# Strassen's seven products on a quarter of K in seven blocks of the last FFN

## The chip, the cores and the metric

The kernel runs on one core of a Trainium2 chip. The metric is the device time of one execution in microseconds, the median of a few runs. The engines are TensorE (PE in the profile, its weight loads PEld), VectorE (DVE), ScalarE (ACT), GpSimd (POOL) and SyncE (SP), which here only issues DMAs. Each works through its own list of instructions in order, and they wait for each other on semaphores.

## The reference

Two layers of a transformer trunk on 256 tokens with 2048 features in float32. Each layer has a token mixer and a SwiGLU FFN with D_FF = 5632. The change touches the FFN of the second layer, and in it the two products with `w1` and `w3`:

```python
def _swiglu(h, w1, w3, w2):
    return (jax.nn.silu(h @ w1) * (h @ w3)) @ w2

for i in range(DEPTH):
    ...
    h = x * (1.0 + sc_f) + sh_f
    y = _swiglu(h, ffn_w1[i], ffn_w3[i], ffn_w2[i])
    x = _layer_norm(DEEPNORM_ALPHA * x + (1.0 + g_f) * y, ln2_g[i], ln2_b[i])
```

## The kernel before

Every product of float32 matrices is made of three products of rounded parts: a matrix is split into a high part (`hi`, type fp32r) and what is left (`lo`), and `hi*hi + lo*hi + hi*lo` is summed in PSUM. The activations are split once. The weights come in **units** of 256 rows of K and 512 columns (512 KB, 128 partitions x 1024 elements), and each goes through a line of stations:

- SP loads it into one of five slots of `raw` (L492), when VectorE has done with the unit five before it (`lo_ready`).
- ScalarE copies it into `whi`, the high part (L710). The rings `whi` and `wlo` have five slots too, so the split of a unit waits until TensorE has used the unit five before it (`units_used`).
- VectorE subtracts: `wlo = raw - whi` (L1167).
- TensorE uses it (`unit`, L1862 and L1868): 2 chunks of K x 2 halves of the tokens x 3 products, 12 matmuls of 128x128 by 512, each with its own weight load.

VectorE and ScalarE count how far TensorE is in `pl.pe`: `units(1)` adds one and splits units until five are ahead. An instruction that comes after `units(n)` in their lists therefore stands behind the split of the unit four ahead of the last one counted.

The FFN takes the 5632 columns in 11 blocks of 512, in two passes (6 and 5 blocks). In a block, 8 units of `w1` are accumulated into one pair of PSUM banks (a bank for each half of the tokens) and 8 units of `w3` into the next; two pairs take turns (`pl.block % 2`), and `pair_read` tells TensorE that a pair was read. After the `w1` half ScalarE applies Silu out of PSUM (L1025); after the `w3` half VectorE multiplies (L1684) and transposes (L1261). SP stores the result to HBM and reads it back by token (L554, L564), ScalarE and VectorE split it (L773, L1266). After each pass follow the units of `ffn_w2` on the transposed `u`, four column blocks, each read by VectorE (L1308, L1299). VectorE also makes the adaLN vectors (`ada`, L1204), one reduction of 2048 elements after every third unit; POOL loads their weights. The last of them fall into block 3 of the second layer's FFN.

Of the kernel before, what the change touches and what calls it, by code (L numbers as in the profile page):

```python
# [7 lines left out]
F32 = mybir.dt.float32  # L8
F32R = mybir.dt.float32r
I32 = mybir.dt.int32  # L10
ALU = mybir.AluOpType
# [59 lines left out]

TOTAL = sum(PROJ) + 1 + 2 * (4 * PAIRS + 3 * D_FF // P * 4 // UC)
LAST_DOWN = TOTAL - 4 * FF_PASSES[-1] * 4 // UC

ADA_HEAD = 2 * KC
# [105 lines left out]
def trunk(nc, A, rows, u_store, qk_store, out):  # L181
# [75 lines left out]
    c_bc = new("c_bc", [P, D])  # L257
    ada_w = new("ada_w", [P, 2, D])
    raw = new("raw", [P, RING, UNIT])
    whi = new("whi", [P, RING, UNIT], F32R)  # L260
# [85 lines left out]
    with ExitStack() as ctx:  # L346
# [14 lines left out]
        ada_half_done = sem("ada_half_done")  # L361
        raw_in = [sem(f"raw_in{i}") for i in range(RING)]
        ln_in = sem("ln_in")
# [77 lines left out]
        piece_summed = sem("piece_summed")  # L441
        piece_out = sem("piece_out")

        block = ctx.enter_context(nc.Block())
# [15 lines left out]
        def split_lo(n):  # L460
            return end_lo[:, n - (TOTAL - STASH), :] if n >= TOTAL - STASH else wlo[:, n % RING, :]

        def ends(layer):
# [8 lines left out]
        def _(sp):  # L472
# [14 lines left out]
            def load(source):  # L487

                s = pl.unit % RING
                if pl.unit >= RING:  # L490
                    sp.wait_ge(lo_ready, pl.unit - RING + 1)
                sp.dma_start(raw[:, s, 0:source.shape[-1]], source).then_inc(raw_in[s], 16)  # L492
                pl.unit += 1
# [64 lines left out]
            def u_back(l, i):  # L558
# [3 lines left out]
                for a in range(QUADS):  # L562
                    for t in range(T):
                        sp.dma_start(rows_of(l, i)[a * QUAD:(a + 1) * QUAD, t, :, :],  # L564
                                     u_store[b % 2][:, :, t, a, :].rearrange("q x s -> x q s")
                                     ).then_inc(u_moved[b % 2], 16)

            def load_ffn(l):
                first = 0
                for nb in FF_PASSES:  # L570
                    for i in range(first, first + nb):
                        if (l, i) == (0, 0):
# [109 lines left out]
        def _(act):  # L682
            pl = Place()

            def widths():
                for layer in range(LAYERS):
                    for k in range(PROJ[layer]):
                        yield UC * unit_width(layer, k)
                        if layer == 1 and k == PAIRS - 1:
                            yield KC * H  # L690
                    for _ in range(4 * PAIRS):
                        yield UNIT
                    for _ in range(3 * D_FF // P * 4 // UC):
                        yield UNIT
            width = list(widths())

            def split():

                s, n = pl.unit % RING, width[pl.unit]
                act.wait_ge(raw_in[s], 16 * (pl.unit // RING + 1))  # L700
                if pl.unit >= TOTAL - STASH:
                    act.wait_ge(units_used, LAST_DOWN)
                elif pl.unit >= RING:
                    act.wait_ge(units_used, pl.unit - RING + 1)
                if pl.unit == narrow:
                    nc.scalar.activation(f_weights(s)[:, :, 0, :], raw[:, s, 0:n].rearrange("p (c n) -> p c n", c=KC),
                                         ACT.Copy).then_inc(hi_ready, 1)
                    pl.unit += 1
                    return
                nc.scalar.activation(split_hi(pl.unit)[:, 0:n], raw[:, s, 0:n], ACT.Copy).then_inc(hi_ready, 1)  # L710
                pl.unit += 1
# [285 lines left out]
            def w_o():  # L997
                units(2 + 2 * PAIRS - SPLIT)
                pl.block += 4

            def ffn(l):
                units(PAIRS - SPLIT if l > 0 else 3)
                first = 0
                for n, nb in enumerate(FF_PASSES):
                    for i in range(nb):
                        silu = silu_of(l, n, i)
                        if (l, n, i) == (0, 0, 1):
# [19 lines left out]
                        if i > 0:  # L1027
                            u_high(l, n, first + i - 1)
                        units(2 if (l, n, i) == (0, 0, 0) else PAIRS)
                        if (n, i) == (0, nb - 1):  # L1030
# [105 lines left out]
        def _(dve):  # L1136
            pl = Place()
            total = sum(PROJ) + 1 + 2 * (4 * PAIRS + 3 * D_FF // P * 4 // UC)

# [9 lines left out]
            def chain(ins):  # L1149
                mark(ins)  # L1150
                own()

            def split():

                s = pl.unit % RING
                n = KC * H if pl.unit == narrow else UNIT
# [3 lines left out]
                if pl.unit == narrow:  # L1160
                    nc.vector.tensor_tensor(f_weights(s)[:, :, 1, :],
                                            raw[:, s, 0:n].rearrange("p (c n) -> p c n", c=KC),
                                            f_weights(s)[:, :, 0, :].bitcast(F32),
                                            ALU.subtract).then_inc(lo_ready, 1)
                    pl.unit += 1
                    return
                nc.vector.tensor_tensor(split_lo(pl.unit)[:, 0:n], raw[:, s, 0:n],  # L1167
                                        split_hi(pl.unit)[:, 0:n].bitcast(F32),
# [47 lines left out]

            def units_with_ada(n, spare=0):

                for k in range(n):
                    units(1)  # L1220
                    if pl.pe % 3 == 0 and k < n - spare:
                        ada()
# [406 lines left out]
            def w_o(layer):  # L1629
# [10 lines left out]
                units(PAIRS - SPLIT - (1 if layer == 0 else 0))  # L1640

            def ffn(l):
                if l > 0:
                    units(PAIRS - SPLIT - T)
                first = 0
                for n, nb in enumerate(FF_PASSES):
                    last = n == len(FF_PASSES) - 1
                    for i in range(nb):
                        if (l, n, i) == (0, 0, 1):
                            units(1)  # L1650
# [20 lines left out]
                        elif (n, i) != (0, 0):  # L1671
                            units_with_ada(PAIRS)
                        pl.block += 1
                        if i > 0:
                            u_low(l, n, first + i - 1)
                        if (l, n, i) == (0, 0, 0):
                            units(1)
                        else:
                            units_with_ada(PAIRS, 2)
                        dve.wait_ge(units_used, pl.pe)  # L1680
# [155 lines left out]
        def _(pe):  # L1836
# [290 lines left out]
            def w_o(layer):  # L2127
# [11 lines left out]
                split_end(parts[PAIRS - SPLIT:], 2 * layer)  # L2139

            def ffn(l):
                made = l * U_BLOCKS
                for n, nb in enumerate(FF_PASSES):
                    for i in range(nb):
                        if (n, i) == (0, 0):
                            norm_turn(2 * l)
# [210 lines left out]
```

## Time and profile before

| | |
|---|---|
| timed runs, median (lowest to highest of 3) | 2195.85 us (2192.31 to 2196.93) |
| profiled execution: its span, first to last instruction | 2191.0 us |
| the profiled execution's own time around the span | not given by the page |
| TensorE busy, of the span | 2139.0 us (98%), 9557 matmuls |
| VectorE busy | 1596.9 us (73%) |
| ScalarE busy | 990.1 us (45%) |
| mean granted TensorE clock | 0.998 |

The page counts an engine as busy while an instruction of it runs; matmuls overlap, so their durations (0.39 us) are longer than their distance. Idle time before an instruction is put down to the engine that released it. The rows below are of the last FFN, from about 1465 us to the end, but for those on the clock, which are of the first 110 us.

### The profile page before, as it was taken

How to read it: one execution, taken by the hardware profiler on the slowest of the kernel's cores; microseconds unless marked ns; L12 is line 12 of the kernel's file. 1: busy time of each engine (PE TensorE's matmuls, PEld its weight loads, DVE VectorE, ACT ScalarE, POOL GpSimd, SP SyncE). 2: the span in 40 equal slices, each digit the busy share in tenths (PEclk: the TensorE clock that was granted, in tenths of full speed). 3: DMA queues.
4: the chain of work that ended last, by engine and by line, in shares of the span. 5: the costliest groups of instructions: out<-in, count | busy, mean ns of one | idle time of the engine just before them, and what ended most of it. 6: DMA issues, size and time to landing. Idle time of an engine off the chain costs nothing.

```text
span 2191.0 us, 24820 instructions
## 1 busy us (share of the span) xinstructions
PE 2139.0 (98%) x9557; PEld 1744.3 (80%) x9557; DVE 1596.9 (73%) x1792; ACT 990.1 (45%) x1291; POOL 105.1 (5%) x208
## 2 busy tenths in 40 slices
PE   5799999999999999999999999999999999999999
PEld 2378887888888888888788888878888888888887
DVE  6789999777777777778877666878775555455566
ACT  1077646444443444443544455554444433444443
POOL 2101100000000000000000000000000000000000
PEclk9999999999999999999999999999999999999999
DMA  9999997889998898999589788958987765666773
GB/s 387 418 364 362 363 388 285 276 292 341 337 340 319 320 340 322 318 350 361 193 287 331 264 273 282 338 175 290 332 295 226 234 194 191 214 212 213 219 239 124
DMA packets 177064, 635.90 MB, mean 290 GB/s; under 512 B 20385, under 2 KB 51377, under 8 KB 150705
## 3 DMA queue, kind: packets, MB, share of 16 engines
q1 hardware_dynamic: 147298, 427.93, 56.0%
q0 software_dynamic: 27792, 201.34, 24.6%
q10 hardware_dynamic: 1856, 5.04, 0.6%
q8 instruction: 76, 1.25, 0.2%
q14 instruction: 42, 0.34, 0.0%
HBM read 616.37 MB, written 17.86 MB: 289 GB/s over the span
## 4 chain that ended last, share of the span: by engine, by line
PE 86%; DMA 6%; DVE 6%; ACT 2%; issue 1%; POOL 0%; ACTq 0%; SPq 0%; DVEq 0%; POOLq 0%
PE ps L1862 53%; PE ps L1868 27%; PE ps L1879 3%; DMA gate<-in_ada_w 3%; DMA raw<-in_mla_w_o 1%; DVE wlo L1167 1%; DMA ada_head<-in_ada_w 1%; DVE ada_w L1204 1%; DVE gate L1204 1%; DMA ada_w<-in_ada_w 1%; DMA raw<-in_mla_w_uv 1%; PE ps L2091 0%; ACT whi L710 0%; DVE ada_head L1204 0%; PE ps L2121 0%
## 5 line engine op out<-in xcount | busy, mean ns | idle before, releaser
L1167 DVE TENSOR_TENSOR wlo<-raw,whi 128x1024 fp32r<-128x1024 f32 (+1 forms) x717 | 867.1, 1216 | 513.8 <-ACT whi L710 512.7
L710 ACT ACTIVATE whi<-raw 128x1024 fp32r<-128x1024 f32 (+1 forms) x717 | 756.1, 1056 | 1033.8 <-PE ps L1868 952.4
L1862 PE MATMUL ps<-whi,hT_hi 128*128 128x512 f32 x1880 | 585.7, 393 | 1.5 <-DVE hT_lo L1595 1.5
L1862 PE MATMUL ps<-whi,hT_lo 128*128 128x512 f32 x1880 | 579.5, 389 | 0.0
L1868 PE MATMUL ps<-wlo,hT_hi 128*128 128x512 f32 x1880 | 502.7, 389 | 0.0
L1862 PEld LDWEIGHTS ps<-whi,hT_lo 128*128 128x128 f32 x1880 | 352.9, 188 | 74.0
L1868 PEld LDWEIGHTS ps<-wlo,hT_hi 128*128 128x128 f32 x1880 | 352.9, 188 | 73.7
L1862 PEld LDWEIGHTS ps<-whi,hT_hi 128*128 128x128 f32 x1880 | 350.1, 188 | 72.9 <-DVE hT_lo L1595 2.0
L1204 DVE CUSTOM_DVE_ANT_0 ada_w<-ada_w,c_bc,cols 128x2048 f32<-128x2048 f32 x145 | 339.8, 2345 | 16.4 <-ACT c_bc L1050 8.4
L1862 PE MATMUL ps<-whi,uT_hi 128*128 128x512 f32 x656 | 202.0, 389 | 0.0
L1862 PE MATMUL ps<-whi,uT_lo 128*128 128x512 f32 x656 | 201.9, 389 | 0.0
L1868 PE MATMUL ps<-wlo,uT_hi 128*128 128x512 f32 x656 | 175.3, 389 | 0.0
L1862 PEld LDWEIGHTS ps<-whi,uT_lo 128*128 128x128 f32 x656 | 123.1, 188 | 25.6
L1862 PEld LDWEIGHTS ps<-whi,uT_hi 128*128 128x128 f32 x656 | 123.1, 188 | 25.6
L1868 PEld LDWEIGHTS ps<-wlo,uT_hi 128*128 128x128 f32 x656 | 123.1, 188 | 25.5
L655 POOL DMA_DIRECT2D ada_w<-in_ada_w x145 | 76.8, 530 | 1289.9 <-DVE mod L1204 1289.1
L2204 PE MATMUL ps<-down_w,h 128*128 128x512 f32 x128 | 64.8, 652 | 28.2 <-ACT h L1063 28.2
L2204 PEld LDWEIGHTS ps<-down_w,h 128*128 128x128 f32 x128 | 25.2, 208 | 57.0 <-ACT h L1063 30.9
L1204 DVE CUSTOM_DVE_ANT_0 ada_head<-ada_head,c_bc,cols 128x2048 f32<-128x2048 f32 x16 | 37.5, 2351 | 10.6 <-DMA ada_head<-in_ada_w 10.3
L1063 ACT ACTIVATE h<-ps,mod 128x256 f32<-128x256 f32 x16 | 8.9, 561 | 74.2 <-DVE mod L1204 54.4
L917 ACT ACTIVATE p_sb<-p_sb,pinv 128x128 f32<-128x128 f32 x64 | 25.7, 452 | 27.9 <-DVE pinv L1623 27.9
L1879 PE MATMUL ps<-whi,hT_hi 128*128 128x512 f32 x72 | 29.8, 414 | 3.3 <-issue 1.6
(274 smaller groups left out, 1470.0 us busy)
## 6 DMA issues: line engine op xcount, KB each, us to landing
raw<-in_ffn_w SPq DMA_DIRECT2D x528, 512.0 KB, 4.7
ada_w<-in_ada_w POOLq DMA_DIRECT2D x145, 1024.0 KB, 7.6
raw<-in_fox_w_in SPq DMA_DIRECT2D x96, 512.0 KB, 5.3
ada_head<-in_ada_w POOLq DMA_DIRECT2D x16, 1024.0 KB, 20.3
raw<-in_mla_w_o SPq DMA_DIRECT2D x32, 512.0 KB, 8.6
raw<-in_fox_w_o SPq DMA_DIRECT2D x32, 512.0 KB, 5.5
gate<-in_ada_w POOLq DMA_DIRECT2D x12, 1024.0 KB, 9.0
ada_low<-in_ada_w POOLq DMA_DIRECT2D x10, 1024.0 KB, 10.4
```

Source lines behind the costliest of these rows:

```text
L655: pool.dma_start(ada_buffer(n), A["ada_w"][l, q, c]).then_inc(ada_in[ADA_SLOT[n]], 16)
L710: nc.scalar.activation(split_hi(pl.unit)[:, 0:n], raw[:, s, 0:n], ACT.Copy).then_inc(hi_ready, 1)
L917: ins = nc.scalar.activation(p_sb[:, g % 2, a:b], p_sb[:, g % 2, a:b], ACT.Copy, scale=pinv[:, g % 2, t:t + 1])
L1063: nc.scalar.activation(h32[:, c, :], ps[:, 4 + c % 2, 0:S], ACT.Identity, scale=mod[:, SC_A, c:c + 1], bias=mod[:, SH_A, c:c + 1]).then_in ...
L1167: nc.vector.tensor_tensor(split_lo(pl.unit)[:, 0:n], raw[:, s, 0:n], split_hi(pl.unit)[:, 0:n].bitcast(F32), ALU.subtract).then_inc(lo_rea ...
L1204: nc.vector.tensor_tensor_reduce(w, w, c_bc[:, :], 1.0, adab_col[:, q, c:c + 1], ALU.mult, ALU.add, mod[:, q, c:c + 1]).then_inc(ada_done, 1)
L1862: nc.tensor.matmul(ps[:, 2 * pair + t, 0:width], a[:, t * P:(t + 1) * P], w_hi, start=(first and c == 0 and a is hi), stop=False)
L1868: ins = nc.tensor.matmul(ps[:, 2 * pair + t, 0:width], hi[:, t * P:(t + 1) * P], w_lo, start=False, stop=(end and c == UC - 1))
L1879: ins = nc.tensor.matmul(ps[:, 2 * pair + t, :], a[:, t * P:(t + 1) * P], w, start=(first and c == 0 and a is hi), stop=(end and c == UC - 1))
L2204: ins = nc.tensor.matmul(ps[:, 2 * which + t, :], h32[:, c, t * P:(t + 1) * P], w[:, which * LORA:(which + 1) * LORA], start=(c == 0), sto ...
```

## The change

In blocks 4 to 10 of the second layer's FFN (the last two of the first pass, all five of the second), the first quarter of K (512 of 2048 rows, two units of `w1` and two of `w3`) is computed by Strassen's scheme. Seen as a 2x2 of blocks, the token halves are rows, the two K units columns of the left matrix; `B11`, `B21` (of `w1`) and `B12`, `B22` (of `w3`) make the right one. Seven products of one token half by one unit take the place of eight. The left sums `S1` to `S4` are made once (`mix_inputs`, in block 3), in the buffer of the adaLN weights, and split by ScalarE and VectorE. The right sums `T1` to `T4` are made in every block by VectorE (`operand_sum`), two units ahead, in the raw slot of one of their terms, and then split like any unit. A block so has 19 units in place of 16: 7 operand units of 6 matmuls and 12 plain units of 12 for the other three quarters of K.

The seven products and the rest need all eight PSUM banks: 0 to 3 for `B11`, `T1`, `T2`, `T3`, the pair 4 and 5 for the `w1` side (with `B21`, `T4` and the plain units), the pair 6 and 7 for the `w3` side (with `B22` and the plain units). ScalarE copies bank 0 and 1 out, VectorE adds the single products together, adds the pairs (left: L1862, right: L1866), ScalarE applies Silu, VectorE multiplies and transposes. New semaphores tell TensorE which bank was read: `first_copied`, `fifth_copied`, `sixth_read`, `left_done`, `right_read`.

Four more raw slots (`raw_more`) lie where `c_bc` and the adaLN weights were; their loads wait for `mix_ready`. The adaLN reductions are made earlier: after every second unit in the first half of block 3, and to the end of block 2. The raw slots are given out by a table (`RAW_SLOT`, `RAW_FREE`), so loads run up to ten units ahead.

```diff
+FAST_FROM = 4
+FAST_BLOCKS = range(FAST_FROM, sum(FF_PASSES))
+OPERANDS = {"B11": (W1, 0), "B12": (W3, 0), "B21": (W1, 1), "B22": (W3, 1)}
+SUM_ON_DVE = {"T1": ("B11", "B12"), "T3": ("B12", "B22"), "T2": ("B11", "B22"), "T4": ("B11", "B21")}
+LEAD = 2
+    return ([("B11", 0), ("B22", 0), ("B21", 0)] + w1[:3] + [("T1", 0), ("T3", 0)] + w1[3:]
+            + [("T2", 0)] + w3[:3] + [("T4", 0)] + w3[3:])
...
@@ SP
+                n = pl.unit
+                if RAW_FREE[n]:
+                    sp.wait_ge(lo_ready, RAW_FREE[n])
+                if RAW_SLOT[n] >= RING:
+                    sp.wait_ge(mix_ready, 1)
+                sp.dma_start(raw_of(n)[:, 0:source.shape[-1]], source).then_inc(raw_in[RAW_SLOT[n]], 16)
...
+            def load_fast(first, i):
+                for n, (kind, j) in enumerate(FAST_UNITS):
+                    if kind in ONTO:
+                        pl.unit += 1
+                        continue
...
+                    load(A[name][1, i * PAIRS + which])
...
+                    if i > first and n == U_OUT_AFTER:
+                        u_out(1, i - 1)
+                    if i > first and n == U_BACK_AFTER:
+                        u_back(1, i - 1)
...
@@ ScalarE
+            def fast_block(n, i):
+                b = i - FAST_FROM
+                units(AT["B11"] + 4)
+                act.wait_ge(units_used, pl.pe - 4)
+                act.wait_ge(u_flipped, U_BLOCKS + i)
+                nc.scalar.activation(silu_all[:, 0, :], ps[:, 0, :], ACT.Copy).then_inc(first_copied, 1)
+                units(AT["T1"] - AT["B11"] - 4)
+                act.wait_ge(units_used, pl.pe)
+                nc.scalar.activation(u[:, 1, :], ps[:, 1, :], ACT.Copy).then_inc(fifth_copied, 1)
...
+                act.wait_ge(left_done, b + 1)
+                nc.scalar.activation(silu_all[:, :, :], silu_all[:, :, :], ACT.Silu).then_inc(fast_silu, 1)
...
@@ VectorE
+            def operand_sum(n):
...
+                if kind == "T1":
+                    dve.wait_ge(raw_in[slot["B12"]], 16 * loads)
+                onto, other = (raw_tile(slot[name]) for name in SUM_ON_DVE[kind])
+                nc.vector.tensor_tensor(onto, onto, other, ALU.add).then_inc(sum_made, 1)
...
+            def fast_block(n, i):
...
+                units(AT["T4"] - AT["T2"] - 1)
+                dve.wait_ge(units_used, pl.pe)
+                own()
+                nc.vector.tensor_tensor(silu_all[:, :, :], silu_all[:, :, :], ps[:, 4:6, :], ALU.add
+                                        ).then_inc(left_done, 1)
+                units(FAST_COUNT - AT["T4"])
+                dve.wait_ge(units_used, pl.pe)
+                nc.vector.tensor_tensor(u[:, :, :], u[:, :, :], ps[:, 6:8, :], ALU.add).then_inc(right_read, 1)
+                dve.wait_ge(right_read, b + 1)
+                dve.wait_ge(fast_silu, b + 1)
+                chain(nc.vector.tensor_tensor(u[:, :, :], silu_all[:, :, :], u[:, :, :], ALU.mult))
+                flip(1, i, u)
...
@@ TensorE
+            def operand(bank, stationary, first, end):
+                s = pl.unit % RING
+                pe.wait_ge(hi_ready, pl.unit + 1)
+                for c, (hi, lo) in enumerate(stationary):
+                    for a in (hi, lo):
+                        nc.tensor.matmul(ps[:, bank, :], a, whi[:, s, c * NB:(c + 1) * NB],
+                                         start=(first and c == 0 and a is hi), stop=False)
...
+            def fast_block(i):
+                b = i - FAST_FROM
+                pair_free(pl.block)
+                pair_free(pl.block + 1)
+                if b == 0:
+                    pe.wait_ge(mix_ready, 1)
+                for kind, j in FAST_UNITS:
...
+                    if kind == "B21":
+                        if b:
+                            pe.wait_ge(left_done, b)
+                        operand(4, rows_of_h(1, 0), True, False)
...
+                    if kind == "B22":
+                        if b:
+                            pe.wait_ge(right_read, b)
+                        operand(6, mixed(S4), True, False)
...
@@ TensorE, before the units of ffn_w2
+                    if l == 1:
+                        done = sum(i < made - U_BLOCKS for i in FAST_BLOCKS)
+                        for read in (first_copied, fifth_copied, sixth_read, left_done, right_read):
+                            pe.wait_ge(read, done)
```

Three places of the engines' lists follow, each in the order in which its engine takes them; line numbers are of the kernel of each. First VectorE at the end of a block, before (L1167 is the low split, L1684 the read of the finished pair, L1261 the transposition):

```order
L1266 TENSOR_TENSOR uT_lo<-u_rows,uT_hi 128x1024 [waits u_high_ready]
L1167 TENSOR_TENSOR wlo<-raw,whi 128x1024 [waits hi_ready] x8
L1684 TENSOR_TENSOR u<-silu,ps 128x512 [waits pair_read1,units_used]
L1684 TENSOR_TENSOR u<-silu,ps 128x512
L1261 STREAM_TRANSPOSE u_squares<-u 128x1024 [waits pair_read0,u_moved1]
```

The same place between two changed blocks, now (L1347 is the low split, L1329 a sum, L1862 and L1866 the adds of the left and the right pair):

```order
L1862 TENSOR_TENSOR silu<-silu,ps 128x1024 [waits dve_step,units_used]
L1347 TENSOR_TENSOR wlo<-raw,whi 128x1024 [waits hi_ready]
L1347 TENSOR_TENSOR wlo<-raw_more_104,whi 128x1024 [waits hi_ready]
L1329 TENSOR_TENSOR raw_more_105<-raw_more_105,raw_more_107 128x1024 [waits raw_in8]
L1347 TENSOR_TENSOR wlo<-raw_more_106,whi 128x1024 [waits hi_ready]
L1866 TENSOR_TENSOR u<-u,ps 128x1024 [waits units_used]
L1869 TENSOR_TENSOR u<-silu,u 128x1024 [waits fast_silu,right_read]
L1441 STREAM_TRANSPOSE u_squares<-u 128x1024 [waits pair_read0,u_moved0,dve_step]
```

The read of the finished right pair stands in the same place as before, behind the low split of the fifth unit of the next block (the third L1347 here). One add of 1024 elements and one product of 1024 have taken the place of two products of 512.

TensorE at a block's start, before (the last unit of a block, then the first of the next product):

```order
L1862 MATMUL ps<-whi,hT_hi 128x512 [waits hi_ready]
L1862 MATMUL ps<-whi,hT_hi 128x512
L1862 MATMUL ps<-whi,hT_lo 128x512 x2
L1862 MATMUL ps<-whi,hT_hi 128x512 x2
...
L1868 MATMUL ps<-wlo,hT_hi 128x512 [waits lo_ready]
L1868 MATMUL ps<-wlo,hT_hi 128x512 x3
L1862 MATMUL ps<-whi,hT_hi 128x512 [waits hi_ready,pair_read0]
```

And now, from the last four matmuls of a changed block to the third unit of the next (`B11`, `B22`, `B21`):

```order
L2409 MATMUL ps<-wlo,hT_hi 128x512 x3
L2386 MATMUL ps<-whi,hT_hi 128x512 [waits first_copied,hi_ready,pair_read0,pair_read1]
L2386 MATMUL ps<-whi,hT_lo 128x512
...
L2390 MATMUL ps<-wlo,hT_hi 128x512 [waits lo_ready]
L2390 MATMUL ps<-wlo,hT_hi 128x512
L2386 MATMUL ps<-whi,s_hi 128x512 [waits hi_ready,right_read]
L2386 MATMUL ps<-whi,s_lo 128x512
...
L2390 MATMUL ps<-wlo,s_hi 128x512 [waits lo_ready]
L2390 MATMUL ps<-wlo,s_hi 128x512
L2386 MATMUL ps<-whi,hT_hi 128x512 [waits hi_ready,left_done]
```

Before, the first unit of a product waits for the read of the pair before last; now the second unit of a block waits for the read of the pair that was just finished.

VectorE where the first changed block follows (L1826 to L1840 make the left sums, L1923 is L1684 of before), now only:

```order
L1826 TENSOR_TENSOR mix_100<-hT_hi,hT_lo 128x1024 [waits ada_done]
L1831 TENSOR_TENSOR s_102<-mix_100 128x256 [waits dve_step]
L1832 TENSOR_TENSOR s_102<-mix_100 128x256
L1834 TENSOR_TENSOR s_102<-s_102,mix_100 128x256 [waits dve_step]
L1835 TENSOR_TENSOR s_102<-s_102,mix_100 128x256 [waits dve_step]
L1347 TENSOR_TENSOR wlo<-raw,whi 128x1024 [waits hi_ready] x2
L1840 TENSOR_TENSOR s_lo<-s_102,s_hi 128x1024 [waits mix_high]
L1347 TENSOR_TENSOR wlo<-raw_more_104,whi 128x1024 [waits hi_ready]
...
L1329 TENSOR_TENSOR raw_more_104<-raw_more_104,raw_more_107 128x1024 [waits raw_in8]
L1347 TENSOR_TENSOR wlo<-raw,whi 128x1024 [waits hi_ready]
L1923 TENSOR_TENSOR u<-silu,ps 128x512 [waits pair_read1,units_used]
```

The five low splits of the changed block's first units and the first sum stand between the mix and the read that frees the last pair of block 3.

## Rows read from the trace of the kernel before

**Rows 1.** The page: span, then busy time, share and instructions of each engine.
```profile
span 2191.0 us, 24820 instructions
PE 2139.0 (98%) x9557; PEld 1744.3 (80%) x9557; DVE 1596.9 (73%) x1792; ACT 990.1 (45%) x1291; POOL 105.1 (5%) x208
```
**Rows 2.** Windows of the last FFN: busy time and instructions, clock, DMA share, GB/s.
```profile
core 0: us, PE busy (x) PEld busy (x) DVE busy (x) ACT busy (x) POOL busy (x), PEclk, DMA share, GB/s
1600.00:1700.00 100.00, 100.00 (x443) 82.81 (x442) 62.63 (x57) 42.84 (x43) 1.58 (x3) 1.00 0.79 252
...
1800.00:1900.00 100.00, 100.00 (x443) 82.81 (x442) 50.48 (x46) 39.64 (x39) 0.00 (x0) 1.00 0.61 194
```
**Rows 3.** Groups by line, 1500 to 2191 us: busy and mean, then idle before them.
```profile
L1167 DVE TENSOR_TENSOR wlo<-raw,whi 128x1024 fp32r<-128x1024 f32 x243 | 296.5, 1223 | 265.7 <-ACT whi L710 265.7
L710 ACT ACTIVATE whi<-raw 128x1024 fp32r<-128x1024 f32 x243 | 257.5, 1060 | 384.3 <-PE ps L1868 380.1 <-DMA raw<-in_ffn_w 4.2
...
L1862 PE MATMUL ps<-whi,hT_hi 128*128 128x512 f32 x648 | 199.5, 389 | 0.0
...
L1204 DVE CUSTOM_DVE_ANT_0 ada_w<-ada_w,c_bc,cols 128x2048 f32<-128x2048 f32 x15 | 35.2, 2346 | 0.0
L1261 DVE STREAM_TRANSPOSE u_squares<-u 128x1024 f32<-128x1024 f32 x11 | 13.7, 1246 | 1.2
```
**Rows 4.** Timeline at the end of block 3: start, duration, engine, line, operation.
```profile
1635.07 1.07 PE L1868 MATMUL ps<-wlo,hT_hi 128*128 128x512 f32 x4
...
1635.97 0.61 PE L1862 MATMUL ps<-whi,hT_hi 128*128 128x512 f32 x2
...
1636.23 1.06 ACT L710 ACTIVATE whi<-raw 128x1024 fp32r<-128x1024 f32 x1 [1.66 <-PE ps L1868]
...
1637.33 1.23 DVE L1167 TENSOR_TENSOR wlo<-raw,whi 128x1024 fp32r<-128x1024 f32 x1 [0.31 <-ACT whi L710]
...
1638.47 1.28 DVE L1684 TENSOR_TENSOR u<-silu,ps 128x512 f32<-128x512 f32 x2
...
1638.69 0.61 PE L1862 MATMUL ps<-whi,hT_hi 128*128 128x512 f32 x2
```
**Rows 5.** Timeline where TensorE waits for VectorE, before the last FFN.
```profile
1464.37 0.42 DVE L1247 TENSOR_TENSOR hT_lo<-tmp,hT_hi 128x256 fp32r<-128x256 f32 x1
...
1464.85 0.50 PE L1879 MATMUL ps<-whi,hT_hi 128*128 128x512 f32 x1 [0.33 <-DVE hT_lo L1247]
...
1465.19 0.39 PE L1879 MATMUL ps<-whi,hT_lo 128*128 128x512 f32 x1
```
**Rows 6.** Timeline of SP's issues at the end of block 3.
```profile
1641.12 0.33 SPq L554 DMA_DIRECT2D u_store<-u_squares  x1
...
1644.39 3.75 SPq L564 DMA_DIRECT2D u_rows<-u_store  x8
```
**Rows 7.** Landing in us: raw loads, one behind the read-back, adaLN loads (page).
```profile
DMA to landing us min/median/max: 3.3/4.2/10.2
...
raw<-in_ffn_w SPq DMA_DIRECT2D x1, 512.0 KB, 5.1
...
ada_w<-in_ada_w POOLq DMA_DIRECT2D x145, 1024.0 KB, 7.6
```
**Rows 8.** Windows of the first stage, columns as in rows 2.
```profile
40.00:50.00 10.00, 10.00 (x37) 5.42 (x37) 7.82 (x8) 1.65 (x3) 1.90 (x4) 1.00 1.02 419
...
66.00:67.00 1.00, 1.00 (x2) 0.48 (x2) 0.68 (x1) 0.00 (x0) 0.12 (x1) 0.50 0.99 410
...
86.00:87.00 1.00, 1.00 (x3) 0.37 (x2) 1.00 (x1) 0.00 (x0) 0.00 (x0) 0.50 1.02 419
```
**Rows 9.** TensorE's timeline in the first stage, idle time before in brackets.
```profile
65.71 6.41 PE L2204 MATMUL ps<-down_w,h 128*128 128x512 f32 x8 [3.78 <-ACT h L1063]
...
84.53 5.40 PE L2204 MATMUL ps<-down_w,h 128*128 128x512 f32 x8 [2.18 <-ACT h L1063]
...
103.67 3.70 PE L2204 MATMUL ps<-down_w,h 128*128 128x512 f32 x8 [2.35 <-ACT h L1063]
```

More of the change, by code:

```diff
@@ new lines, with raw_slots, take @@
+UNIT_KINDS = unit_kinds()
+assert len(UNIT_KINDS) == TOTAL
+FAST_START = next(n for n, kind in enumerate(UNIT_KINDS) if kind)
+def raw_slots():
+    slots, free, count, beside = [], [], [], {}
+    last, loads, sums = [-1] * RAWS, [0] * RAWS, collections.Counter()
+    held = {}
+    def take():
+        return min((s for s in range(RAWS) if s not in held.values()), key=lambda s: last[s])
+    for n, kind in enumerate(UNIT_KINDS):
+        if n < FAST_START:
+            s = n % RING
+        else:
+            s = held[ONTO[kind]] if kind in ONTO else take()
+        slots.append(s)
+        free.append(last[s] + 1)
+        counter, key = (sums, "DVE") if kind in SUM_ON_DVE else (loads, s)
+        counter[key] += 1
+        count.append(counter[key])
+        last[s] = n
+        if kind in HELD_UNTIL:
+            held[kind] = s
+        if kind == "B21":
+            b = take()
+            loads[b] += 1
+            beside[n] = b, last[b] + 1, loads[b]
+            last[b] = n
+            held["B12"] = b
+        for name, by in HELD_UNTIL.items():
+            if by == kind:
+                last[held.pop(name)] = n
+    return slots, free, count, beside
@@ L1137, in _ @@
             pl = Place()
[L1138 removed]
+            total = TOTAL
             def mark(ins):
@@ L2139, in w_o @@
                 split_end(parts[PAIRS - SPLIT:], 2 * layer)
+            def operand(bank, stationary, first, end):
[5 more added lines that the diff above has]
+                                         start=(first and c == 0 and a is hi), stop=False)
+                pe.wait_ge(lo_ready, pl.unit + 1)
+                for c, (hi, lo) in enumerate(stationary):
+                    ins = nc.tensor.matmul(ps[:, bank, :], hi, wlo[:, s, c * NB:(c + 1) * NB],
+                                           start=False, stop=(end and c == UC - 1))
+                ins.then_inc(units_used, 1)
+                pl.unit += 1
@@ new lines, in plain_unit @@
+            def plain_unit(pair, j, first, end):
+                s = pl.unit % RING
+                parts = [(hT_hi[:, UC * j + c, :], hT_lo[:, UC * j + c, :]) for c in range(UC)]
+                pe.wait_ge(hi_ready, pl.unit + 1)
+                for c, (hi, lo) in enumerate(parts):
+                    for a in (hi, lo):
+                        for t in range(T):
+                            nc.tensor.matmul(ps[:, 2 * pair + t, :], a[:, t * P:(t + 1) * P],
+                                             whi[:, s, c * NB:(c + 1) * NB],
+                                             start=(first and t == 1 and c == 0 and a is hi), stop=False)
+                pe.wait_ge(lo_ready, pl.unit + 1)
+                for c, (hi, lo) in enumerate(parts):
+                    for t in range(T):
+                        ins = nc.tensor.matmul(ps[:, 2 * pair + t, :], hi[:, t * P:(t + 1) * P],
+                                               wlo[:, s, c * NB:(c + 1) * NB], start=False,
+                                               stop=(end[t] and c == UC - 1))
+                ins.then_inc(units_used, 1)
+                pl.unit += 1
```

186 lines of the change are left out of this document (169 added, 17 removed).

## The prediction

> **What bounds the kernel now.** I read the page's busy shares first: TensorE is busy 98% of the span, VectorE 73%, ScalarE 45% [rows 1]. A busy TensorE alone says little, so I looked at the stretch that the change touches, in windows: between 1600 and 1900 us TensorE is busy for all of every 100 us, with 443 matmuls in each and the full clock, while VectorE works 50 to 63 us of 100 and ScalarE about 41 [rows 2]. The groups of lines of the last FFN say the same from the other side: the matmuls of L1862 waited for nothing (0.0 us idle), VectorE's low split waited 265.7 us for ScalarE's high split, and that one 380.1 us for TensorE [rows 3]. So in this stage both splitting engines sit behind TensorE, and only two things move the end: matmuls taken away, or TensorE made to wait.
>
> The timeline around a block's end gives the clockwork [rows 4]. One unit starts at 1635.97 and the next at 1638.69: 2.72 us for 12 matmuls, 0.2267 us each. Counted from the moment at which TensorE starts the unit after a block's last (1635.97), ScalarE begins its next high split at +0.26, VectorE its low split at +1.36, and VectorE's first read of the finished block (L1684) at +2.50, done at +3.78. TensorE does not feel this late read, because the next product goes into the other pair of PSUM banks.
>
> **What is removed.** A block of 16 units has 192 matmuls. The changed block has 12 plain units of 12 and 7 operand units of 6, so 186. Seven blocks save 42 matmuls, 42 x 0.2267 = 9.5 us. All else is cost.
>
> **The added waits.** The changed block uses all eight banks at once: 0 to 3 for single products, 4 and 5 for the left pair, 6 and 7 for the right pair. Its second unit, B22, writes bank 6 and waits for right_read, that is, for VectorE's add L1866 of the block before. In VectorE's order that add stands behind the low split of the next block's fifth unit. This split needs ScalarE's high split, which needs the ring slot that the block's last unit gives back. So the add starts at +2.50 like L1684 now, not when the banks are full. Its length is bounded by two PSUM reads of 512 (1.28 us together, [rows 4]) and one of 1024 from SBUF (1.22, [rows 3]); I take 1.22. TensorE wakes 0.06 us after the releasing VectorE instruction (1464.37 + 0.42 to 1464.85) and loses 0.11 us more on its first matmul (0.34 to the next start, where 0.23 is usual) [rows 5]. B22 so starts at 2.50 + 1.22 + 0.06 = +3.78. It was due after the six matmuls of B11, at +1.36. The stall is 3.78 - 1.36 + 0.11 = 2.53 us, at the five places where a changed block follows a changed one: 12.7 us.
>
> At four other places nothing stands between. Into the first changed block of either pass, B11 waits for both pairs, the just finished one too; from the last changed block of either pass, the first unit of ffn_w2 waits for right_read. There the stall is the full 3.9 us (2.50 + 1.22 or 1.28 + 0.06 + 0.11). At the very first it is longer. The loads of its operands go to new buffers that lie where the adaLN weights were, and they wait for mix_ready, which comes late in block 3: the four adaLN reductions of its first half at 2.35 us each [rows 3] between low splits put VectorE at about +24 us of the block, the mix and three splits at about +34, s_lo at +35. Six loads must land before the split ahead of the freeing read: 3.3 us for the first (the least landing time, [rows 7]) and 5 x 1.25 us more for 0.52 MB each at the 419 GB/s that the early stage shows [rows 8], so +44.6; then 1.06 + 1.14 + 1.28 + 0.06 = +48.1, against the block's end at +43.5. That is a stall of 4.7 us with the restart, and 1.5 us more if an adaLN load lands as late as its median of 7.6 us allows [rows 7]. I take 5.5, with 3.9 and 8 as bounds. The four together: 5.5 + 3.9 x 3 = 17.2 us.
>
> **What hides.** Per block VectorE gets three low splits and four sums more, about 1.14 us each back to back, and some 5 us of adds in place of L1684's: 13 us on about 22 of 43.5. It stays at 35 of 42, and the splits run four units ahead, so I price these at nothing. The cover fails where operand units follow each other and TensorE eats a unit in 1.36 us; the longest such run is three, and after it come three plain ones. If it were gone, TensorE would wait for lo_ready, 1.1 us per late split. The three extra high splits (1.06 us) fit ScalarE's 59 free us in 100. DMA bytes are unchanged. One queue matters: SP loads eight units ahead now, so it reaches the store of u before that exists and stands there until the transposition is done, 1.2 + 1.25 us after the add, about +6.3 [rows 3]; everything behind it waits too. The unit that is eighth in TensorE's order is loaded right behind, the next only after the 3.3 us of the store and 3.75 us of eight read-back issues [rows 6], at about +13.4. Landing in 5.1 us as behind such reads now [rows 7], it is split at +19.6, and TensorE wants it at +20.2. That is 0.6 us of slack, so nothing, but a landing at the longest 10.2 us would cost 4.5 us a block.
>
> So far: 12.7 + 17.2 - 9.5 = +20.4 us.
>
> The trace of now shows the late read at +2.50 and no wait of TensorE for it [rows 3, 4]. The Trainium skill (Perfetto Trace Analysis, Optimizing Tensor Performance) says why: independent matmul groups should rotate through different PSUM banks, so that one's evacuation overlaps the next group's matmuls. The same page (Matmul Optimizations) also asks that all eight banks be used. The change follows the second and breaks the first. By the second alone the sum would be -9.5 us, by the first it is +20.4; the late read in the rows decides for the first.
>
> **The clock.** A stalled TensorE can lose its clock. In the first stage a group of eight matmuls takes 3.70 us. After an idle time of 3.78 us it took 6.41, after one of 2.18 us 5.40, and after one of 2.35 us 3.70 [rows 9]; the granted clock was 0.50 in the slow stretches, 1.2 instead of 2.4 GHz [rows 8]. So a fall costs 2.71 or 1.70 us. The five short stalls lie between a gap that cost 1.70 and one that cost nothing: half, 5 x 0.85 = 4.3 us. The four long ones are like the gap of 3.78; I take 2.2, the mean of the two falls, since the fall was not always dear: 8.8 us. Together +13, with bounds of 0 and 9 x 2.71 = 24.
>
> **Sum.** +20.4 + 13 = +33.4 us. The page gives the profiled execution's span, 2191.0 us, and no other time for it; the median of the three timed runs is 2195.85, so 4.85 us lie around the span. 2191.0 + 33.4 + 4.85 = 2229 us.
>
> **Rivals.**
> 1. The stalls come and the clock holds. For it: gaps of 2.35 us and less that kept it. Against: the gap of 3.78 that did not, in a stage with a busier TensorE around it here. 2195.85 + 20.4 = 2216 us. Chance 0.16.
> 2. The clock falls at all nine. The gap of 2.18 us speaks for it, that of 2.35 against. 4 x 2.71 + 5 x 1.70 = 19.3, so 2236 us. Chance 0.12. The Trainium skill (TensorE: Matmul & The Clock Gate, A second HAM failure mode) reports this for short TensorE idles between groups that cycle PSUM banks. By that rule all nine fall; the trace agrees for two gaps of three.
> 3. The loads behind the store of u come late. The slack of 0.6 us speaks for it; the landing of 5.1 us in the same place now against it. About 2 us at five blocks on top of the forecast: 2239 us. Chance 0.10.
> 4. Not slower: VectorE reads the right pair as soon as the last matmul is done, so the read is not tied to the split. Then the add starts at +0.26 and ends at +1.48, B22 loses 0.3 us at five places and the four other places 1.7 each, 8.3 us against 9.5: 2195 us. It decides if the add comes to VectorE before +0.3; it would need VectorE to be past the fifth split by then. VectorE's order, and the +2.50 in the trace, speak against it. Chance 0.03.
>
> **How the numbers follow.** The forecast has 0.56; what is left, 0.03, is a mishap that I don't see. Low end: no falls and 3.9 us at the first block, 2195.85 + 18.8 = 2214.6, rounded down to 2213. High end: all falls at 2.71 and 8 us at the first block, 2195.85 + 20.4 + 2.5 + 24.4 = 2243, taken as 2244. About 0.2 of 100%, some 4 us, is what a measurement here can tell from no change. Only rival 4 lies there or below: faster 0.01, same 0.02, slower 0.97.
>
> **What would show it.** In the profile after: TensorE idle at nine places, released by VectorE, five of about 2.4 us at the second unit of a block and four of 3.8 us or more; L1866 starting 2.5 us after the last unit's end; a granted clock of 0.5 for a few us behind some of them; the block-to-block distance about 44.7 us plus the clock's share, where it is 43.5 now; matmuls fewer by 42. Wrong would be: no TensorE wait for right_read, a wait for lo_ready or for a raw load as the largest, or a granted clock of 1.00 all along.

## The result

The changed kernel takes 2232.38 us (median of 5, 2230.19 to 2234.41), the kernel before 2195.85 in the same runs: 1.0172 times as long, 95% interval 1.0159 to 1.0184. That is 36.5 us more, where 33 were forecast. It is slower although it does less arithmetic.

The page of the changed kernel (the same lines as [rows 1]):

```profile
span 2231.4 us, 25017 instructions
PE 2143.2 (96%) x9515; PEld 1744.7 (78%) x9515; DVE 1688.2 (76%) x1882; ACT 1018.2 (46%) x1320; POOL 105.1 (5%) x208
```

9557 matmuls have become 9515: the 42 are gone. TensorE's busy time has still grown by 4 us, so some of the rest ran slower, and its share of the span fell from 98 to 96%, so it waits. Windows, columns as in [rows 2], show both:

```profile
1645.00:1650.00 5.00, 1.15 (x3) 0.98 (x4) 4.89 (x6) 0.31 (x1) 0.00 (x0) 0.50 0.00 0
...
1695.00:1700.00 5.00, 3.06 (x9) 2.39 (x10) 4.93 (x5) 1.45 (x2) 0.00 (x0) 0.76 0.01 3
...
1970.00:2070.00 100.00, 93.27 (x409) 76.24 (x408) 80.98 (x74) 49.31 (x50) 0.00 (x0) 1.00 0.54 198
```

The 443 matmuls per 100 us of before are 409 here, at the full clock, with TensorE idle for 6.7 us of the 100. In the first two stretches the mean granted clock is 0.50 and 0.76: TensorE works for a while at 1.2 GHz. Who TensorE waited for in the last FFN (line waited for: total, times, longest, in us):

```profile
PE ps L2386 <- DVE u L1866: 11.2, 5, 2.2
PE ps L2386 <- DVE u L1923: 10.8, 1, 10.8
PE ps L2101 <- DVE u L1866: 8.0, 2, 4.0
PE ps L2386 <- issue: 3.7, 1, 3.7
```

Nine waits, 33.7 us, at the nine places named. The kernel before has none there. "issue" is the start of block 6, where the trace shows no releaser; there the missing read is that of ffn_w2's last product, by its place in the program (experiment 5 has the same wait, with that read, L1308, as its releaser). The timeline of one short wait, between blocks 8 and 9, answers to [rows 4]:

```profile
2014.64 1.07 PE L2409 MATMUL ps<-wlo,hT_hi 128*128 128x512 f32 x4
...
2015.55 0.39 PE L2386 MATMUL ps<-whi,hT_hi 128*128 128x512 f32 x1
...
2015.81 1.06 ACT L848 ACTIVATE whi<-raw_more 128x1024 fp32r<-128x1024 f32 x1 [1.66 <-PE ps L2409]
...
2016.45 0.61 PE L2390 MATMUL ps<-wlo,hT_hi 128*128 128x512 f32 x2
2016.90 1.23 DVE L1347 TENSOR_TENSOR wlo<-raw_more,whi 128x1024 fp32r<-128x1024 f32 x1 [0.36 <-ACT whi L848]
...
2018.05 1.21 DVE L1866 TENSOR_TENSOR u<-u,ps 128x1024 f32<-128x1024 f32 x1
...
2019.32 0.50 PE L2386 MATMUL ps<-whi,s_hi 128*128 128x512 f32 x1 [2.25 <-DVE u L1866]
2019.65 0.40 PE L2386 MATMUL ps<-whi,s_lo 128*128 128x512 f32 x1
...
2022.21 0.61 PE L2403 MATMUL ps<-whi,hT_hi 128*128 128x512 f32 x2
```

Count from 2015.55, where B11 starts. ScalarE's high split begins at +0.26, VectorE's low split at +1.35, its add at +2.50, and B22 at +3.77: the clockwork of [rows 4], with TensorE now at the end of it.

### The profile page after: what moved, and what is told of

Its sections match the earlier page's. It is cut to its first block, busy times and chain, and to the rows that moved or that the text cites. A ratio compares the mean times of both kernels' runs of the same rounds, so it can differ in the third digit from the quotient of the medians.

```text
span 2231.4 us, 25017 instructions
## 1 busy us (share of the span) xinstructions
PE 2143.2 (96%) x9515; PEld 1744.7 (78%) x9515; DVE 1688.2 (76%) x1882; ACT 1018.2 (46%) x1320; POOL 105.1 (5%) x208
## 4 chain that ended last, share of the span: by engine, by line
PE 84%; DVE 6%; DMA 6%; ACT 2%; issue 1%; SPq 0%; POOL 0%; ACTq 0%; DVEq 0%; POOLq 0%
PE ps L2101 43%; PE ps L2107 22%; PE ps L2403 7%; DMA ada_head<-in_ada_w 4%; PE ps L2409 3%; PE ps L2118 3%; PE ps L2386 2%; DVE wlo L1347 1%; PE ps L2390 1%; DVE ada_w L1384 1%; ACT whi L848 1%; DMA raw<-in_ffn_w 1%; DVE ada_head L1384 1%; DMA ada_w<-in_ada_w 1%; DMA raw<-in_mla_w_uv 0%
## 5 line engine op out<-in xcount | busy, mean ns | idle before, releaser
L848 ACT ACTIVATE whi<-raw 128x1024 fp32r<-128x1024 f32 (+1 forms) x638 | 671.7, 1056 | 902.3 <-PE ps L2107 710.0
L1347 DVE TENSOR_TENSOR wlo<-raw,whi 128x1024 fp32r<-128x1024 f32 (+1 forms) x638 | 770.1, 1215 | 376.4 <-ACT whi L848 374.4
L2101 PE MATMUL ps<-whi,hT_hi 128*128 128x512 f32 x1432 | 448.4, 394 | 3.7 <-DVE hT_lo L1775 3.7
L2101 PE MATMUL ps<-whi,hT_lo 128*128 128x512 f32 x1432 | 442.6, 390 | 0.0
L2107 PE MATMUL ps<-wlo,hT_hi 128*128 128x512 f32 x1432 | 383.3, 390 | 0.0
L2101 PEld LDWEIGHTS ps<-whi,hT_lo 128*128 128x128 f32 x1432 | 269.3, 188 | 56.7
L2107 PEld LDWEIGHTS ps<-wlo,hT_hi 128*128 128x128 f32 x1432 | 269.2, 188 | 56.4
L2101 PEld LDWEIGHTS ps<-whi,hT_hi 128*128 128x128 f32 x1432 | 266.3, 188 | 57.7 <-DVE hT_lo L1775 4.3
L1347 DVE TENSOR_TENSOR wlo<-raw_more,whi 128x1024 fp32r<-128x1024 f32 x100 | 122.1, 1224 | 81.0 <-ACT whi L848 79.7
L848 ACT ACTIVATE whi<-raw_more 128x1024 fp32r<-128x1024 f32 x100 | 105.7, 1060 | 137.4 <-PE ps L2107 64.5
L2403 PE MATMUL ps<-whi,hT_hi 128*128 128x512 f32 x336 | 103.8, 390 | 0.0
L2403 PE MATMUL ps<-whi,hT_lo 128*128 128x512 f32 x336 | 103.5, 389 | 0.0
L2409 PE MATMUL ps<-wlo,hT_hi 128*128 128x512 f32 x336 | 89.8, 389 | 0.0
```

Of the source, the lines that this page charges most:

```text
L848: nc.scalar.activation(split_hi(pl.unit)[:, 0:n], raw_of(pl.unit)[:, 0:n], ACT.Copy).then_inc(hi_ready, 1)
L1347: nc.vector.tensor_tensor(split_lo(pl.unit)[:, 0:n], raw_of(pl.unit)[:, 0:n], split_hi(pl.unit)[:, 0:n].bitcast(F32), ALU.subtract).then_i ...
L2101: nc.tensor.matmul(ps[:, 2 * pair + t, 0:width], a[:, t * P:(t + 1) * P], w_hi, start=(first and c == 0 and a is hi), stop=False)
L2107: ins = nc.tensor.matmul(ps[:, 2 * pair + t, 0:width], hi[:, t * P:(t + 1) * P], w_lo, start=False, stop=(end and c == UC - 1))
L2403: nc.tensor.matmul(ps[:, 2 * pair + t, :], a[:, t * P:(t + 1) * P], whi[:, s, c * NB:(c + 1) * NB], start=(first and t == 1 and c == 0 and ...
L2409: ins = nc.tensor.matmul(ps[:, 2 * pair + t, :], hi[:, t * P:(t + 1) * P], wlo[:, s, c * NB:(c + 1) * NB], start=False, stop=(end[t] and c ...
```

## The experiments

Seven kernels were run. The first four were compared with the kernel before at 2193.31 us on their chip, the last three at 2193.26. The kernel before took 2.5 us more in the runs beside the changed kernel, so a ratio compares better with 1.0172 than a median with 2232.38.

**1. The add first.** VectorE's part of the changed kernel:

```
-units(FAST_COUNT - AT["T4"])
+units(FAST_COUNT - AT["T4"] - 1)
+pl.pe += 1
 dve.wait_ge(units_used, pl.pe)
 nc.vector.tensor_tensor(u[:, :, :], u[:, :, :], ps[:, 6:8, :], ALU.add).then_inc(right_read, 1)
+ahead()
```

> Edit: in the changed kernel VectorE's add of the right pair stands ahead of the low split of the next block's fifth unit instead of behind it; nothing else. Theory A (the place in VectorE's queue sets the stall): the add can start at +0.03 instead of +2.50 and be done at +1.28, before B22 is due at +1.36. The five short stalls (2.25 us idle and 0.11 us restart each, 11.8 us) go, the two into ffn_w2 shrink from 4.0 to about 1.4 us (5.2 us), the two clock falls behind short stalls go (3.2 us), and if a gap of 1.4 us keeps the clock also the two into ffn_w2 (4.7 us). From 2232 to between 2207 and 2212 us. The waits into blocks 4 and 6 stay. Theory B (TensorE waits for something else that is late at the same time, loads or the left pair): the wait turns up under another name, gain under 4 us, above 2228 us.

Measured: 2208.43 us, 1.0070 of before (1.0056 to 1.0083). TensorE's waits in the last FFN and, below, one block's start:

```profile
PE ps L2388 <- DVE u L1925: 10.9, 1, 10.9
PE ps L2388 <- issue: 3.7, 1, 3.7
PE ps L2103 <- DVE u L1867: 3.5, 2, 1.8
```

```profile
1999.89 0.39 PE L2388 MATMUL ps<-whi,hT_hi 128*128 128x512 f32 x1
2000.09 1.22 DVE L1867 TENSOR_TENSOR u<-u,ps 128x1024 f32<-128x1024 f32 x1 [0.34 <-PE ps L2411]
...
2001.37 0.50 PE L2388 MATMUL ps<-whi,s_hi 128*128 128x512 f32 x1
...
2002.36 1.22 DVE L1347 TENSOR_TENSOR wlo<-raw_more,whi 128x1024 fp32r<-128x1024 f32 x1
```

The add takes the same 1.2 us, but starts at +0.20 instead of +2.50, and B22 starts at +1.48, with the 0.11 us of a first matmul behind a wait and no idle time. The five short waits are gone and the two into ffn_w2 have fallen from 4.0 to 1.8 us. The low split now comes 1.1 us later than in the changed kernel (+2.47 instead of +1.35), and nobody waits for it. Theory B is out: one instruction's place in VectorE's queue is worth about 1% of the time, 22 us by the two ratios (24 by the medians).

**2. TensorE's waits.** Nothing is read earlier; TensorE waits for the banks it is about to write:

```
-pair_free(pl.block + 1)              # at the block's start
+pair_free(pl.block + 1)              # before T3 instead
-operand(0, rows_of_h(0, 0), ...)     # B11; T1, T2, T3 from 1, 2, 3
+operand(2, rows_of_h(0, 0), ...)     # to 3, 0, 1; the readers likewise
-for read in (first_copied, fifth_copied, sixth_read, left_done, right_read):
+for read in (first_copied, fifth_copied, sixth_read):   # the other two 3 units later
```

> Edit: VectorE's order stays as in the changed kernel; TensorE waits for less. The single products swap banks (B11 and T1 in 2 and 3, T2 and T3 in 0 and 1), so that block 4 and block 6 start in banks that were read long ago and wait for the just finished pair only before T3, their eighth unit; into ffn_w2 TensorE waits for the reads of banks 0 to 3 alone, and for those of 4 to 7 three units later. Theory A (the four long stalls are waits for banks that the next unit does not write): into ffn_w2 twice 4.0 + 0.11 us and a clock fall of about 2.3 us go (12.9 us), into block 6 3.7 + 0.1 + 1.5 us (5.3 us), and into block 4 some 5 of the 10.8 us, the rest being late loads. From 2232 to about 2209 us (2205 to 2214). The five short stalls stay at 2.25 us. Theory B (those stalls end on the loads or on u anyway): waits for hi_ready or lo_ready take their places, above 2222 us.

Measured: 2207.34 us, 1.0062 (1.0049 to 1.0076).

```profile
PE ps L2386 <- DVE u L1866: 11.2, 5, 2.2
PE ps L2403 <- ACT whi L848: 2.9, 2, 2.4
PE ps L2409 <- DVE wlo L1347: 0.8, 1, 0.8
```

The five short waits stand to the tenth. Into ffn_w2 and into block 6 nothing is waited for any more, although VectorE still reads as late as before: those three waits were for banks that the next unit does not write. Of the first wait (10.8 us) 3.7 us are left in three pieces, all for split weights, so theory B has this much. The first, 0.5 us, is a high split that waited for a load. The second, 0.8 us, is a low split that stood in VectorE's list behind the late read, its transposition and a sum. The third, 2.4 us, is the tenth unit of block 4, whose load was issued behind the read-back of u: that is what rival 3 of the prediction names.

**3. The loads of the first changed block.** The order of the four added buffers is turned, and their loads wait for less:

```
-sp.wait_ge(mix_ready, 1)
+sp.wait_ge(ada_done, len(ADA_ORDER))   # the first two
+sp.wait_ge(mix_summed, 1)              # the other two
```

> Edit: of the four added raw buffers the first two used now lie where the second adaLN buffer was and wait for the last adaLN reduction alone, the other two for the left sums (the two operands' sum of high and low parts is read by then), instead of all four for s_lo. Theory A (the first stall of 10.8 us is the four loads that wait for mix_ready, and behind them in SP's queue the next ones): loads start 4 to 13 us earlier, the low split of the fifth unit is again bound by the freed ring slot, the stall falls to 3.9 us like the others: 2225 us. Theory B (VectorE or ScalarE are late in block 3 whatever the loads do): stall above 8 us, 2229 us or more.

Measured: 2226.17 us, 1.0148 (1.0132 to 1.0163).

```profile
PE ps L2393 <- DVE u L1873: 11.2, 5, 2.2
PE ps L2393 <- issue: 8.1, 2, 4.4
PE ps L2108 <- DVE u L1873: 8.0, 2, 4.0
```

The first wait fell from 10.8 to 4.4 us (the other "issue" wait is the 3.7 us into block 6). So 6.3 us of it came from the loads that stood behind `mix_ready`. What remains is about the late read that the other long waits share (3.7 to 4.0 us).

**4. The three together**, and block 3's product ahead of the split too.

> Edit: the three edits together (the add first, TensorE's waits, the loads), and also block 3's product L1923 ahead of the low split. Theory A (the whole loss is the nine waits and the clock falls behind them; the 42 matmuls are saved all the same): 33.7 us of waits, 1 us of restarts and 11.3 us of clock go from 2232, which is 2186 us, 9.5 us below the kernel before. Theory B (with the waits gone something hidden decides, VectorE's 22 busy us of 43.5 with the sums, or SP's queue behind the store of u): new TensorE waits for lo_ready or loads, 2195 us or more.

Measured: 2185.92 us, 0.9965 of before (0.9952 to 0.9977). This beats both kernels.

```profile
PE 2131.8 (98%) x9515; PEld 1737.0 (80%) x9515; DVE 1685.4 (77%) x1882; ACT 1016.3 (47%) x1320; POOL 105.5 (5%) x208
```

```profile
PE ps L2414 <- ACT whi L855: 0.8, 1, 0.8
```

```profile
1697.39 0.73 PE L2414 MATMUL ps<-whi,hT_hi 128*128 128x512 f32 x2 [0.75 <-ACT whi L855]
```

```profile
1970.00:2070.00 100.00, 99.93 (x439) 81.87 (x438) 82.83 (x76) 51.90 (x53) 0.00 (x0) 1.00 0.58 213
```

With the same matmuls, splits and sums as the changed kernel, TensorE is busy for 99.9 of 100 us at full clock (93.3 above), and one wait of 0.8 us is left. VectorE works 83 us of 100 and still holds nothing up. The wait that is left is rival 3 again: the tenth unit of block 5 was loaded behind the read-back of u (issued at 1691.22, its high split started at 1696.28), and without the stall before B22 TensorE wants it earlier. So theory B has one wait of 0.8 us, and the time is theory A's. The gain is 7.4 us of the 9.5 that 42 matmuls are worth, and the interval (5 to 10.5 us) holds the whole.

**5. The waits alone.** In the kernel before, without any Strassen, TensorE waits at the nine places for the pair that was just finished:

```
+if l == 1 and made - U_BLOCKS + i >= 4:   # start of blocks 4 to 10
+    pair_free(pl.block + 1)
+if l == 1:                                # both times into ffn_w2
+    pair_free(pl.block + 1)
```

> Edit: the kernel before, all sums and blocks as they were, but at the nine places (the starts of blocks 4 to 10, both times into ffn_w2) TensorE waits for the pair that was just finished. No Strassen: only the wait is added. Theory A (a wait for the late read costs what the long stalls of the changed kernel cost): nine idle times of 3.7 to 4.0 us with 0.11 us of restart, 35 us, and behind each a clock fall of 1.5 to 2.4 us as in the changed kernel, 18 us: 2193 + 53 = 2246 us. Theory B (the clock falls there came from the half-size matmul groups and sums around them): the idle times alone, 2228 us.

Measured: 2247.11 us, 1.0241 (1.0224 to 1.0258).

```profile
PE ps L1862 <- DVE u L1684: 29.3, 8, 3.7
PE ps L1862 <- DVE tmp L1308: 3.7, 1, 3.7
```

```profile
1640.00:1645.00 5.00, 3.15 (x9) 2.54 (x10) 3.04 (x4) 0.00 (x0) 0.00 (x0) 0.77 0.86 271
1645.00:1650.00 5.00, 5.00 (x21) 4.02 (x21) 1.23 (x1) 1.77 (x2) 0.00 (x0) 0.89 0.16 53
1650.00:1655.00 5.00, 5.00 (x24) 4.14 (x23) 2.45 (x2) 1.68 (x3) 0.00 (x0) 1.00 0.70 229
```

The waits sum to 33.0 us, the loss is 53.9. The windows show where most of the other 21 come from: the first wait ends at 1641.85, and from 1645 to 1650 TensorE is busy all the time, yet gets 21 matmuls done at a clock of 0.89, and 24 in the next 5 us at 1.00. Such a dip stands behind each of the nine waits. So a wait of this length costs six tenths as much again, and Strassen's half-size units have no part in it.

**6. The wait met one unit later.** In the changed kernel's list of units B21 comes before B22:

```
-[("B11", 0), ("B22", 0), ("B21", 0)]
+[("B11", 0), ("B21", 0), ("B22", 0)]
```

> Edit: the changed kernel with B22 and B21 swapped in TensorE's order, so that the unit which needs the right pair is the third of a block and is due at +2.72 instead of +1.36; VectorE's add keeps its place. Theory A (the read ends at +3.76 whatever TensorE does): the five short waits shrink by one unit, from 2.25 to 0.9 us, 6.8 us in all; the two clock falls behind them (3.2 us) go if a gap of 0.9 us keeps the clock. From 2232 to 2222 us, or 2225 with the falls. Theory B (TensorE's wait is for the ring or the weights, and moves with the unit): the wait stays at 2.25 us, 2232 us.

Measured: 2220.44 us, 1.0121 (1.0106 to 1.0136).

```profile
PE ps L2386 <- issue: 12.9, 2, 9.2
...
PE ps L2386 <- DVE u L1866: 4.4, 5, 0.9
```

```profile
1690.00:1700.00 10.00, 9.12 (x41) 7.20 (x40) 9.57 (x9) 4.25 (x4) 0.00 (x0) 1.00 0.20 62
```

The five short waits shrink by exactly one half-size unit, from 2.25 to 0.88 us, so the moment of the read is fixed on VectorE's side and TensorE's order only decides how much of it is felt. The clock stays at 1.00 behind all five. The first wait, which the edit does not aim at, is 9.2 us here instead of 10.8.

**7. The waits, with an early read.** Experiment 5, and VectorE's product ahead of the split as in experiment 1:

> Edit: e5_before_waits, and VectorE's product L1684 from block 3 on stands ahead of the low split of the fifth unit to come. Again no Strassen. Theory A (place in the queue sets the stall; gaps under 2 us keep the clock): eight idle times of about 1.75 us, as in e1_add_first, one of 3.7 us into block 6 whose read is not moved, nine restarts of 0.11 us and one fall of 1.5 us: 14 + 3.7 + 1 + 1.5 = 20 us, 2213 us. Theory B (any idle time of TensorE drops the clock): eight falls more of about 1.6 us, 2226 us.

Measured: 2214.72 us, 1.0096 (1.0081 to 1.0111).

```profile
PE ps L1866 <- DVE u L1687: 11.8, 8, 2.1
PE ps L1866 <- DVE tmp L1308: 3.7, 1, 3.7
```

```profile
1640.00:1645.00 5.00, 4.59 (x20) 3.82 (x21) 3.03 (x4) 1.06 (x1) 0.00 (x0) 1.00 0.79 258
1685.00:1690.00 5.00, 4.39 (x19) 3.67 (x20) 3.03 (x4) 1.44 (x2) 0.00 (x0) 1.00 0.67 229
```

Eight waits of 3.66 us have become one of 2.13 and seven of 1.38, and behind none of them does the clock fall; it falls behind the one of 3.66 us into block 6 alone. Against experiment 5 the waits are 17.5 us shorter and the kernel 32.4 us faster: the rest is the clock.

## Why the prediction was right

**The bound** was read rightly: in the last FFN only matmuls and TensorE's waits move the end. Experiment 4 removed the waits and got the matmuls' gain; experiment 5 added waits alone and got a loss, 53.9 us, without any Strassen.

**The 42 matmuls** are 42, and the steady distance between two reads of the right pair is 44.72 us (1973.33 to 2018.05) where 44.7 was forecast.

**What hides** was hidden: none of the nine waits of the last FFN is for split weights or a raw load, with VectorE busy for 34.66 us of a steady block's 44 (1975 to 2019, 35 of 42 forecast).

**The five short waits**: forecast 2.53 us each with the restart, measured 2.58 by the same count: B22 starts at +3.77 where it was due at +1.36, and the 12 matmuls from there take 2.89 us (2019.32 to 2022.21) in place of 2.72. The idle time of the trace is 0.16 us less, 2.25, since it begins where the last matmul's 0.39 us end, and the next was due 0.23 us after that one's start. The part that was not in the trace of before, the length of an add over two banks at once, was taken as 1.22 us and is 1.21. The add starts at +2.50 as L1684 did. Experiments 1 and 6 show the reason that was given: the place behind the low split.

**The four long waits.** Three were forecast at 3.9 us with the restart and are 4.0, 3.7 and 4.0 idle, 4.3, 4.0 and 4.3 by the same count. They need not have been there: the banks that follow were free (experiment 2). The prediction took them as part of the change and came within 0.4 us of their price.

**The first long wait is the term that was mis-sized**: 5.5 us forecast with bounds of 3.9 and 8, measured 10.8 idle, 11.1 by the same count and outside the bounds. The chain was the right one, and three links of it were short. In the changed kernel's block 3, timeline with the idle time before in brackets:

```profile
1594.41 0.62 PE L2101 MATMUL ps<-whi,hT_hi 128*128 128x512 f32 x2
...
1621.43 1.06 ACT L848 ACTIVATE whi<-raw 128x1024 fp32r<-128x1024 f32 x1 [6.66 <-DMA raw<-in_ffn_w]
...
1632.86 1.22 DVE L1840 TENSOR_TENSOR s_lo<-s,s_hi 128x1024 fp32r<-128x1024 f32 x1
...
1634.11 1.28 SPq L603 DMA_DIRECT2D raw_more<-in_ffn_w  x3
...
1637.76 1.06 ACT L848 ACTIVATE whi<-raw_more 128x1024 fp32r<-128x1024 f32 x1 [6.07 <-DMA raw_more<-in_ffn_w]
...
1644.25 1.06 ACT L848 ACTIVATE whi<-raw 128x1024 fp32r<-128x1024 f32 x1 [0.22 <-DMA raw<-in_ffn_w]
1645.21 1.22 DVE L1329 TENSOR_TENSOR raw_more<-raw_more,raw_more 128x1024 f32<-128x1024 f32 x1
1646.34 1.22 DVE L1347 TENSOR_TENSOR wlo<-raw,whi 128x1024 fp32r<-128x1024 f32 x1
1647.48 1.28 DVE L1923 TENSOR_TENSOR u<-silu,ps 128x512 f32<-128x512 f32 x2
1648.85 0.77 PE L2386 MATMUL ps<-whi,hT_hi 128*128 128x512 f32 x1 [10.76 <-DVE u L1923]
```

Block 3 begins at 1594.41, and its 192 matmuls end at +43.5. s_lo is done at +39.7 instead of +35: ScalarE had waited 6.66 us for a raw load, so high splits, u and the mix slid back together. (The change moves the last adaLN reductions closer together; whether that made this load late was not tried.) The six loads took 10.1 us to the last split's start, where 9.6 were forecast. And a sum (L1329) that stands between the split and the read was not counted: 1.1 us. So B11 starts at +54.4 and not at +48.1. Experiment 3 shows that the loads' wait was the heart of it: 6.3 us.

**The clock** was forecast at 13 us with bounds of 0 and 24. Against the steady block the falls cost 2.0, 1.6, 2.4, 1.6, 1.6 and 2.3 us in order, about 11.4 in sum: it fell behind all four long waits and behind two of the five short ones. That it would fall behind the four long ones and behind half of the short ones was a guess between two rows; that it came so near is luck in part. The Trainium skill (TensorE: Matmul & The Clock Gate, A second HAM failure mode) reports a kernel whose clock oscillates because of short idles between groups of matmuls that cycle through PSUM banks. Read as a rule for every such idle, as in rival 2, it would have fallen behind all nine; here it held behind three.

**The sum.** 33.7 us of idle time, 9 x 0.16 = 1.4 that the idle time leaves out, 1.4 of restarts (0.15 each), 11.4 of clock, less 9.5: 38.4 us, where 33.4 were forecast. The first wait was 5.6 us too small in the forecast, the three other long ones 0.9, the five short ones 0.2, and the clock 1.7 too large. The two profiled spans differ by 40.4; 1.95 us of that lie ahead of the last FFN already (its first read starts at 1507.9 before and 1509.9 after) and are not the change's: that read starts at 1510.0 in experiment 5 too, whose program is the kernel before up to there. So the last FFN of the profiled execution lost 38.4 us, as the sum has it. The 36.5 us between the medians are less, and the profiled execution was the slowest of the five, 2.0 us above their median. The 4.85 us that the forecast puts around the span are a reading of two different executions: where a time and its own span are both on record, 1.7 to 3.2 us lie between them. In the forecast the term goes in and out again and changes nothing.

**The rivals.** The clock did not hold (1) and did not fall everywhere (2). No load behind the store of u was waited for (3): the high split that was forecast to be done at +19.6 was done at +17.7 (2033.27, counted from 2015.55), and TensorE began the unit at +20.3:

```profile
2028.39 0.43 SPq L603 DMA_DIRECT2D raw<-in_ffn_w  x1
...
2032.21 1.06 ACT L848 ACTIVATE whi<-raw 128x1024 fp32r<-128x1024 f32 x1 [4.67 <-DMA raw<-in_ffn_w]
...
2035.81 0.61 PE L2403 MATMUL ps<-whi,hT_hi 128*128 128x512 f32 x2
```

The wait of B22 is part of that slack. In experiments 2 and 4, where waits ahead of the unit are gone, TensorE does wait for it, once in each (2.4 and 0.8 us). A read at once (4) was not what the kernel did; experiment 1 made it do so and the price came out near what that rival had, 1.8 us idle into ffn_w2 where 1.7 was worked out.

## What to carry to other kernels

When a change lets one block use every accumulator bank, look at who reads the last bank and what stands ahead of that read in its engine's queue: a read that cost nothing in the old order becomes a wait for everything that stands ahead of it. Let the engine that must wait do so for the banks it is about to write, not for all that were in use, and put the freeing read ahead of work whose result is needed several units later. Here that turned a loss of 1.7% into a gain of 0.35% with the same arithmetic.

## What was not expected of the hardware

How long TensorE waited went with whether it lost its clock in this stage. In experiments 1, 6 and 7 there were fifteen waits of 0.88 to 2.13 us, and behind none was the granted clock below 1.00. Of all waits of 3.66 us and more in these kernels, 24 in number, not one kept it. No wait here lies between 2.38 and 3.66 us. The waits of 2.25 us went either way: two of five fell in the changed kernel, in experiment 2 and in experiment 3, each time into blocks 5 and 7 and never into 8, 9 and 10. What sets those two apart from the other three was not found; a wait of 2.38 us in experiment 2 kept the clock as well, and in the first stage of the kernel before one of 2.18 us lost it and one of 2.35 us kept it [rows 9]. So length alone does not decide there. A fall behind a wait of 2.25 us cost some 1.6 us in the changed kernel, so the price of such a wait rises by two thirds where the clock goes.
